# Attention of two decoder layers with its output written already turned, negated logits, four logit buffers and 64-row score tiles

## The chip, the cores and the metric

The kernel runs on one core of a Trainium2 chip. The metric is the device time of one execution in microseconds (us), lower is better. The kernel before takes 1696.79 us, the median of 3 runs (1696.77 to 1696.97). All data are 32-bit floats.

## The reference

One program computes two models one after the other on a sequence of 256 positions of 1024 columns, here worked in two tiles of 128 positions: a first block (feed-forward, three kinds of attention, feed-forward), and then two layers, each with a mixed attention, a cross attention to a memory, and a convolved feed-forward. Only the mixed attention of these two layers and the cross attention behind it are touched. Per layer, from a projection `h` of the input:

```
# latent attention (unit kind M below): 8 heads, causal, values of 64 columns
s = (q_nope . k_nope + q_rope . k_rope) * 96 ** -0.5
o_a = softmax(s where key <= query) @ v
# sparse attention: 8 heads of 64 columns in 2 key groups, three branches
s_c = q . k_compressed * 64 ** -0.5 - slope * distance     # K: 15 compressed keys
s_s = q . k_slc * 64 ** -0.5 - slope * distance            # S: selected keys (all blocks, at 256 positions)
s_w = q . k_win * 64 ** -0.5 - slope * distance            # W: window keys (all, at 256 positions)
o_b = g0 * softmax(s_c) @ v_c + g1 * softmax(s_s) @ v_s + g2 * softmax(s_w) @ v_w
x = layer_norm(ALPHA * x + concat(o_a, o_b) @ w_out)       # 1024 columns
# cross attention (X): 4 heads of 256 columns, 256 memory keys
x = layer_norm(ALPHA * x + softmax(q . k_mem / 16) @ v_mem @ wo)
```

## The kernel before

The kernel names engines directly: each engine has a program of its own, written out in order, and semaphores between them. TensorE (PE) multiplies and transposes, VectorE (DVE) adds biases, takes maxima and divides, ScalarE (ACT) takes exponentials and copies out of PSUM. Large products are worked in a 2 x 2 block scheme of seven products (numbered 1 to 7), whose sums of weights DVE makes.

The mixed attention of a layer is a list of 26 units, UNITS_2: K of tile 0, K of tile 1, then for each tile S0 W0 S1 W1 S2 W2 S3 W3 M0 M1 M2 M3. A unit is one kind, two heads (K: eight) and one tile of 128 queries; in tile 0 it has 128 keys, in tile 1 it has 256. The function `attend` stands three times, once in the program of each engine, and runs over steps j:

- PE (L1180): scores of unit j (L1190), the transposition of the probabilities of unit j-2 (L1206), the product with the values of unit j-3 (L1232). The result is 128 queries x 64 columns for each head, in PSUM.
- DVE (L2322): `logits(j)` adds the bias and takes the row maximum in one instruction for each head (L2357, a custom instruction, with a short one that reads the maximum), then negates the maxima (L2360); `mid` works only for K, B and X units (for X, reciprocal L2378 and two scalings of the probabilities L2382); `output(j-3)` takes the reciprocal of the row sum (L2403), multiplies it with the gate for S and W (L2413), and scales the result out of PSUM into the rows O1 (L2421), for S and W adding to what stands there (L2419).
- ACT (L1678): copies the transposed probabilities of unit j-2 out of PSUM (L1702), then the exponentials of unit j (L1692), each with a short instruction that reads the row sum.

Scores have two buffers in PSUM, logits three in SBUF (`lbuf`), transposed probabilities two in PSUM and two in SBUF (PTS). In the first steps PE also computes quarters of the memory values (L1538), eight passes of 512 columns each. In the trace each product of 32-bit floats shows as two records, a transposition as one.

When the units are done, PE transposes the rows O1 to columns x_t (batches E_O, L1116), ACT copies them out (L1603, L1609), and `shared_product` (L831) multiplies them with w_out: products 1 and 2 need only tile 0, the others need also sums that DVE makes of both tiles (`act_sums_of`). Cross attention runs four units X through the same `attend`.

## Time and profile before

| | |
|---|---|
| median of 3 runs | 1696.79 us |
| the profiled execution | 1696.81 us |
| its span | 1694.9 us |
| TensorE clock granted, of full | 0.998 |
| PE busy | 1665.5 us (98%) |
| PE weight loads busy (beside PE) | 1281.4 us (76%) |
| DVE busy | 1223.2 us (72%) |
| ACT busy | 352.5 us (21%) |
| POOL busy | 212.7 us (13%) |

The profile is one execution. The span goes from the first to the last instruction, and some 1.9 us of the execution's time lie around it. Busy time of PE counts each matmul from its start to a modelled end, so that short waits of PE between two matmuls do not show as idle; the distance between starts shows them. The mixed attention of layer 0 runs from 831.11 to 891.98 us, that of layer 1 from 1312.19 to 1373.05 us.

### The profile page before, as it was taken

The numbers are of one execution on the slowest core, as the hardware profiler recorded it, in microseconds if no ns is written. First come the engines' busy times: TensorE is split into PE (matmuls) and PEld (weight loads), VectorE is DVE, ScalarE is ACT, GpSimd is POOL, SyncE is SP. The second block draws the span as 40 slices with busy tenths as digits, with TensorE's granted clock in tenths as the row PEclk, the third lists the DMA queues.
The fourth block names the chain that finished last, engine by engine and source line by source line (L and its number), as shares of the span: only waits on it lengthen the run. The fifth ranks groups of instructions, "written<-read, shape, count | busy, mean of one in ns | idle before, by whom it ended". The sixth has DMA issues, their size and how long they took to land.

```text
span 1694.9 us, 22817 instructions
## 1 busy us (share of the span) xinstructions
PE 1665.5 (98%) x8726; PEld 1281.4 (76%) x8726; DVE 1223.2 (72%) x2230; ACT 352.5 (21%) x893; POOL 212.7 (13%) x139
## 2 busy tenths in 40 slices
PE   7999999999999999999999999999999999999998
PEld 6887488877847886477784969994687767699953
DVE  6777467976787777573376778996844685789995
ACT  2111000034511111112270212220012531222210
POOL 1222211121021212211001000002120000000021
PEclk9999999999999999999999999999999999999999
DMA  9685454524176555346513536444447206265440
GB/s 320 194 230 177 146 199 162 175 80 149 51 232 213 160 164 184 124 145 178 207 51 131 155 125 194 156 170 153 158 121 252 100 1 224 71 226 177 150 173 25
DMA packets 163755, 267.07 MB, mean 158 GB/s; under 512 B 4279, under 2 KB 106477, under 8 KB 163519
## 3 DMA queue, kind: packets, MB, share of 16 engines
q1 hardware_dynamic: 157902, 248.66, 43.8%
q0 software_dynamic: 5008, 15.91, 3.3%
q8 instruction: 70, 1.15, 0.3%
q10 hardware_dynamic: 736, 1.05, 0.3%
q14 instruction: 39, 0.31, 0.1%
HBM read 262.52 MB, written 2.03 MB: 156 GB/s over the span
## 4 chain that ended last, share of the span: by engine, by line
PE 90%; DVE 5%; DVEq 2%; issue 1%; ACT 1%; DMA 1%; SPq 0%; ACTq 0%
PE psum L1017 19%; PE psum L886 16%; PE psum L1065 13%; PE psum L952 12%; PE psum L844 7%; PE psum L1275 4%; PE psum L1481 3%; PE psum L1538 3%; PE psum L1190 3%; PE psum L1116 3%; PE psum L1232 2%; PE psum L825 2%; PE psum L1104 2%; PE psum L1206 1%; PE psum L1221 1%
## 5 line engine op out<-in xcount | busy, mean ns | idle before, releaser
L695 POOL TENSOR_TENSOR work<-ring,work 128x1024 f32<-128x1024 f32 (+2 forms) x59 | 147.4, 2499 | 791.5 <-DVE work L2199 791.5
L2191 DVE TENSOR_TENSOR work<-ring 128x1024 f32<-128x1024 f32 (+2 forms) x102 | 122.0, 1196 | 83.3 <-PE psum L1065 74.3
L1065 PE MATMUL psum<-ring,work 128*128 128x512 f32 x352 | 160.8, 592 | 0.0
L2195 DVE TENSOR_TENSOR ring<-ring 128x1024 f32<-128x1024 f32 (+2 forms) x104 | 131.7, 1267 | 7.7
L2199 DVE TENSOR_TENSOR work<-ring 128x1024 f32<-128x1024 f32 (+2 forms) x102 | 122.6, 1202 | 7.6
L1065 PEld LDWEIGHTS psum<-ring,work 128*128 128x128 f32 x352 | 66.4, 190 | 81.1 <-issue 79.9
L1065 PE MATMUL psum<-work 128*128 128x512 f32 x264 | 122.5, 592 | 0.0
L1017 PE MATMUL psum<-x_t,work 128*128 128x128 f32 x832 | 101.4, 275 | 0.0
L1017 PE MATMUL psum<-work,ring 128*128 128x128 f32 x832 | 101.4, 275 | 0.0
L1017 PE MATMUL psum<-x_t,ring 128*128 128x128 f32 x832 | 97.4, 275 | 1.6 <-ACT x_t L1610 1.6
L1017 PEld LDWEIGHTS psum<-x_t,work 128*128 128x128 f32 x832 | 97.1, 192 | 0.0
L1017 PEld LDWEIGHTS psum<-work,ring 128*128 128x128 f32 x832 | 97.1, 192 | 0.0
L1017 PEld LDWEIGHTS psum<-x_t,ring 128*128 128x128 f32 x832 | 95.0, 192 | 2.4 <-issue 2.4
L1065 PEld LDWEIGHTS psum<-work 128*128 128x128 f32 x264 | 49.7, 190 | 62.0 <-issue 60.3
L2823 DVE SCALAR_TENSOR_TENSOR work<-work 128x254 f32<-128x254 f32 (+1 forms) x176 | 83.5, 526 | 3.3
L886 PE MATMUL psum<-ring,work 128*128 128x256 f32 x352 | 83.2, 379 | 0.0
L886 PE MATMUL psum<-ring,x_t 128*128 128x256 f32 x352 | 81.7, 386 | 1.5 <-DMA ring<-in_ffn_w_gate_dram 1.3
L886 PE MATMUL psum<-work,x_t 128*128 128x256 f32 x352 | 82.9, 379 | 0.0
L1190 PE MATMUL psum<-work 128*128 128x256 f32 (+2 forms) x384 | 79.5, 338 | 0.3 <-DVE stat L2360 0.3
L886 PEld LDWEIGHTS psum<-ring,x_t 128*128 128x128 f32 x352 | 67.9, 194 | 12.2 <-DMA ring<-in_ffn_w_gate_dram 2.4
L1692 ACT ACTIVATE work<-work,stat 128x256 f32<-128x256 f32 (+1 forms) x136 | 61.6, 453 | 66.5 <-DVE stat L2360 65.6
L886 PEld LDWEIGHTS psum<-ring,work 128*128 128x128 f32 x352 | 66.9, 190 | 9.1
(304 smaller groups left out, 2865.6 us busy)
## 6 DMA issues: line engine op xcount, KB each, us to landing
ring<-in_ffn_w_up_dram SPq DMA_DIRECT2D x66, 1024.0 KB, 7.9
ring<-in_w_in_dram SPq DMA_DIRECT2D x21, 2048.0 KB, 7.9
ring<-in_ffn_w_down_dram SPq DMA_DIRECT2D x20, 2048.0 KB, 7.8
ring<-in_ffn_w_gate_dram SPq DMA_DIRECT2D x22, 1024.0 KB, 5.7
ring<-in_xa_wkv_dram SPq DMA_DIRECT2D x8, 2048.0 KB, 9.5
ring<-in_w_out_dram SPq DMA_DIRECT2D x6, 2048.0 KB, 10.9
ring<-in_xa_wq_dram SPq DMA_DIRECT2D x4, 2048.0 KB, 7.9
ring<-in_xa_wo_dram SPq DMA_DIRECT2D x4, 2048.0 KB, 11.3
```

Source lines behind the costliest of these rows:

```text
L695: nc.gpsimd.tensor_tensor(t4, quarters(n, chunks, pitch)[2], t2, ALU.subtract).then_inc(fourth_ready, 1)
L844: last = mm(share_bank(p), acts[p][:, q, :], rhs[:, i, :], start=(q == 0), stop=(q == KD // 2 - 1))
L886: last = mm(corners(j)[p], acts[p][:, i, :], rhs[:, i, :], start=(i == 0), stop=(i == KD // 2 - 1))
L952: last = mm(row_corners(j)[p][:, 0:pitch // 2], acts[p][:, i, :], rhs[:, i, :], start=(i == 0), stop=(i == KD // 2 - 1))
L1017: last = mm(corners(j)[p][:, c * P:(c + 1) * P], weights[:, i, c * P:(c + 1) * P], acts[p][:, i, :], start=(i == 0), stop=(i == KD // 2 - 1))
L1065: last = mm(sums[p], acts[p][:, q, :], rhs[:, i, :], start=(q == 0), stop=(q == KF // 2 - 1))
L1190: last = mm(PS[:, o:o + x["keys"]], q, k[:, 0:x["keys"]], start=(c == 0), stop=(c == len(pairs) - 1))
L1275: last = mm(row_corners(q + 1)[p], acts_of_gates[p][:, i, :], rhs[:, i, :], start=(i == 0), stop=(i == KD // 2 - 1))
L2191: v.tensor_tensor(t3, b22, b12, ALU.subtract)
L2195: v.tensor_tensor(b12, b12, b11, ALU.subtract)
L2199: v.tensor_tensor(t2, b22, b12, ALU.subtract).then_inc(forms_ready, 1)
L2823: last = v.scalar_tensor_tensor(dst, UP[:, q, 0:T - t], CWT[:, 2 - t, k:k + 1], dst, ALU.mult, ALU.add)
```

## The change

It changes the mixed attention in five ways. (1) The gates and the division by the row sum are put on the probabilities, before they are transposed (`mid`), for all kinds. (2) The product with the values takes the values as the stationary operand and the transposed probabilities as the moving one, for two units at a time: 64 output partitions for each head, so two heads write the halves 0..63 and 64..127 of the partitions. K, S and W of a tile add up in PSUM, and ACT copies the finished 512 columns straight into x_t; the rows O1, their transpositions and `turn_mixed` are gone. (3) The custom instruction gives the negated logits and their minimum, which is the bias of the exponential (scale -1), and L2360 is gone; this holds for X as well. (4) The logits have four buffers, and PE's transposition comes three steps behind the scores instead of two (`ahead=3`), the values four; K of tile 1 stands between the tiles. (5) In tile 1 the scores of S and W of the same heads are issued together, each head with 64 rows instead of 128 (`scores_by_rows`), into four PSUM banks.

On PE in tile 1 of a layer, before, one unit after the other (L1190 scores, L1206 transpositions, L1232 values):

```order
L1190 MATMUL psum<-work 128x256 x2
L1206 MATMUL psum<-ident_fours,work 128x128 x4
L1232 MATMUL psum<-work 128x64 x4
L1190 MATMUL psum<-work 128x256 x2
L1206 MATMUL psum<-ident_fours,work 128x128 x4
L1232 MATMUL psum<-work 128x64 x4
```

and after, S and W (L1196 the scores by rows, L1227 transpositions, L1250 values by halves), first with K of tile 1 (L1238), then the round of S and W as it repeats:

```order
L1227 MATMUL psum<-ident_fours,work 128x128 x4
L1238 MATMUL psum<-work 128x128 x4
L1196 MATMUL psum<-work 128x256 x4
L1227 MATMUL psum<-ident_fours,work 128x128 x8
L1250 MATMUL psum<-work 64x128 x8
L1196 MATMUL psum<-work 128x256 x4
```

Two units now go through PE as one round, and the number of instructions is the same.

At the end of a layer's attention PE has before:

```order
L1206 MATMUL psum<-ident_fours,work 128x128 x4
L1232 MATMUL psum<-work 128x64 x4
L1206 MATMUL psum<-ident_fours,work 128x128 x4
L1232 MATMUL psum<-work 128x64 x8
L1116 MATMUL psum<-ident_fours,work 128x128 x8
L844 MATMUL psum<-ring,x_t 128x512 x4
L1116 MATMUL psum<-ident_fours,work 128x128 x8
```

and after (L848 is the first product of `shared_product`):

```order
L1211 MATMUL psum<-work 128x256 x2
L1227 MATMUL psum<-ident_fours,work 128x128 x4
L1250 MATMUL psum<-work 64x128 x8
L1227 MATMUL psum<-ident_fours,work 128x128 x8
L1250 MATMUL psum<-work 64x128 x8
L1227 MATMUL psum<-ident_fours,work 128x128 x4
L1250 MATMUL psum<-work 64x128 x8
L848 MATMUL psum<-ring,x_t 128x512 x8
```

The sixteen transpositions L1116 are gone, and the values of the last four units come in two lots of eight.

On DVE a unit of tile 1 before (ISA is the custom instruction and its read):

```order
L2357 ISA work,stat<-psum,work 128x256
L2357 ISA stat 128x1
L2357 ISA work,stat<-psum,work 128x256
L2357 ISA stat 128x1
L2360 TENSOR_SCALAR stat<-stat 128x2
L2403 RECIPROCAL stat<-stat 128x2
L2421 TENSOR_SCALAR work<-psum,stat 128x64 x2
```

and after:

```order
L2413 ISA work,stat<-psum,shared 128x256
L2413 ISA stat 128x1
L2413 ISA work,stat<-psum,shared 128x256
L2413 ISA stat 128x1
L2446 RECIPROCAL stat<-stat 128x2
L2457 TENSOR_SCALAR work<-work,stat 128x256 x2
```

The reciprocal now belongs to the unit two steps back, and what follows it scales the probabilities and stands ahead of their transposition.

The core of the diff:

```diff
 def unit(kind, n, tile):
...
+UNITS_2 = [x for i in range(TT) for x in
+           [unit("K", 0, i)] + [unit(k, h, i) for h in range(4) for k in "SW"] + [unit("M", h, i) for h in range(4)]]
+SPARSE_UNITS, TILE_UNITS = 9, 13
...
-            return w(W_L + 512 * (u % 3), 512)
+            return w((W_L, W_L + 512, W_L + 1024, W_O1)[u % 4], 512)
...
 # PE
+                def scores_by_rows(j):
+                    u = u0 + j
+                    pe.wait_ge(group_free, at(H_WV + 2, G_LAYER, l))
+                    pe.wait_ge(logits_ready, at(u, U2, l))
+                    for t in (j, j + 1):
+                        x = units[t]
+                        for s in range(2):
+                            r = slice(HD * s, HD * s + HD)
+                            o = ((u0 + t) % 2) * 1024 + s * x["pitch"]
+                            (q, k), = query(x, s, 1)
+                            last = mm(PS[:, o:o + x["keys"]], q[r], k[r, 0:x["keys"]], start=True, stop=True)
+                        last.then_inc(scores_ready, 1)
...
+                def turned_values(j):
...
+                    if k == "K":
+                        if x["tile"]:
+                            pe.wait_ge(unit_done, at(U1 + SPARSE_UNITS, U2, l))
+                        for c in range(4):
+                            last = mm(PO[:, c * P:(c + 1) * P], VBD[:, c // 2, (c % 2) * P:(c % 2 + 1) * P],
+                                      PTS[:, u % 2, (c // 2) * P:(c // 2 + 1) * P], start=(c == 0), stop=False)
...
+                    for t in (j - 1, j):
+                        y = units[t]
+                        o = (512 if k == "M" else 0) + P * y["n"]
+                        for kb in range(y["nk"]):
+                            for s in range(2):
+                                n = s * y["nk"] + kb
+                                last = mm(PO[HD * s:HD * s + HD, o:o + P], values(y, s, kb), PTS[:, (u0 + t) % 2, n * P:(n + 1) * P], ...
+                    last.then_inc(values_ready, 2)
...
-                for j in range(n + 3):
+                for j in range(n + ahead + 1):
...
                     if j < n:
                         scores(j)
-                    if 0 <= j - 2 < n:
-                        turn(j - 2)
+                    if 0 <= j - ahead < n:
+                        turn(j - ahead)
...
-                        value(j - 3)
+                        value(j - ahead - 1)
...
-                attend(UNITS_2, U1, l, {1 + 2 * i + h: values_between(i, h) ...})
+                attend(UNITS_2, U1, l, {1 + 2 * i + h: values_between(i, h) ...}, ahead=3)
...
-                shared_product(L_OUT, ..., E_O, turn_mixed(E_O, U1 + TT + 12, 19, l), l)
+                shared_product(L_OUT, ..., "O", lambda i: None, l)
 # ACT
-                            last = activation(v, v, ACT.Exp, bias=NM[:, b4, s:s + 1], accum_out=SM[:, b4, s:s + 1])
+                            last = activation(v, v, ACT.Exp, scale=-1.0 if x["kind"] in "SWMX" else 1.0, ...
...
+                def turned_rows_out(j):
+                    act.wait_ge(values_ready, at(u + 1, U2, l))
+                    i, sparse = x["tile"], x["kind"] == "W"
+                    src = PO[:, 0:512] if sparse else PO[:, 512:1024]
+                    dst = XT[:, 4:8, i * P:(i + 1) * P] if sparse else XT[:, 0:4, i * P:(i + 1) * P]
...
-                    if 0 <= j - 2 < n:
-                        out_of_psum(j - 2)
+                    if 0 <= j - ahead < n:
+                        out_of_psum(j - ahead)
...
                         exps(j)
...
+                    if 0 <= j - ahead - 1 < n and units[j - ahead - 1]["kind"] in "WM" and units[j - ahead - 1]["n"] == 3:
+                        turned_rows_out(j - ahead - 1)
...
-                turned_rows(E_O, XT, l)
 # DVE
+                                last = v.tensor_tensor_reduce(out=dst, in0=src, in1=bias_of(x, s), scale=-1.0, scalar=-TAKEN,
+                                                              op0=ALU.add, op1=ALU.min, accum_out=NM[:, b4, s:s + 1])
...
+                    if x["kind"] in "SW":
+                        c = 3 * 2 * x["n"] + (1 if x["kind"] == "S" else 2)
+                        for s in range(2):
+                            last = v.tensor_scalar(L[:, s * n:(s + 1) * n], L[:, s * n:(s + 1) * n], RC[:, b4, s:s + 1],
+                                                   ngate[:, x["tile"], c + 3 * s:c + 3 * s + 1], ALU.mult, ALU.mult)
...
+                    if x["kind"] in "MX":
...
-                    if 0 <= j - 1 < n and j != mid_first:
-                        mid(j - 1)
+                    if 0 <= j - ahead + 1 < n and j != mid_first:
+                        mid(j - ahead + 1)
```

For K, `mid` now also takes the reciprocal, multiplies it with the gate and multiplies the probabilities with it: three more small instructions.

## Rows read from the trace of the kernel before

**Rows 1.** The page's chain that ended last, by engine.

```profile
PE 90%; DVE 5%; DVEq 2%; issue 1%; ACT 1%; DMA 1%; SPq 0%; ACTq 0%
```

**Rows 2.** Windows, layer 0's mixed attention, tile 0 and tile 1: length, busy by engine.

```profile
831.11:863.78 32.67, 31.56 (x165) 21.83 (x164) 17.48 (x105) 14.73 (x57) 0.00 (x0) 1.00 0.36 129
863.78:891.98 28.20, 28.20 (x210) 26.17 (x210) 22.13 (x121) 22.02 (x71) 0.00 (x0) 1.00 0.01 1
```

**Rows 3.** Timeline, tile 0: start us, length us, engine, line, operation, tiles, count.

```profile
850.84 0.61 PE L1190 MATMUL psum<-work 128*128 128x128 f32 x4
...
859.23 0.66 PE L1190 MATMUL psum<-work 128*128 128x128 f32 x4
...
859.80 0.28 DVE L2357 CUSTOM_DVE_ANT_0 work<-psum,shared 128x128 f32<-128x128 f32 x1
...
860.01 0.29 DVE L2357 CUSTOM_DVE_ANT_0 work<-psum,shared 128x128 f32<-128x128 f32 x1
...
860.75 0.66 PE L1190 MATMUL psum<-work 128*128 128x128 f32 x4
```

**Rows 4.** Timeline, tile 1, one step of 256 keys.

```profile
877.50 1.08 PE L1190 MATMUL psum<-work 128*128 128x256 f32 x4
...
878.41 0.60 PE L1206 MATMUL psum<-ident_fours,work 128*128 128x128 f32 x4
...
878.62 0.42 DVE L2357 CUSTOM_DVE_ANT_0 work<-psum,work 128x256 f32<-128x256 f32 x1
...
878.85 1.00 PE L1232 MATMUL psum<-work 128*128 128x64 f32 x8
...
878.96 0.42 DVE L2357 CUSTOM_DVE_ANT_0 work<-psum,work 128x256 f32<-128x256 f32 x1
...
879.69 1.08 PE L1190 MATMUL psum<-work 128*128 128x256 f32 x4
```

**Rows 5.** Timeline, products into 32 output partitions each, and the next full ones.

```profile
801.82 1.95 PE L1493 MATMUL psum<-ring,work 128*32 128x128 f32 x64
803.70 0.70 PE L1481 MATMUL psum<-work,ring 128*128 128x256 f32 x2
```

**Rows 6.** Timeline, the first block: full products, two products of 64 rows, transpositions.

```profile
390.19 0.59 PE L1275 MATMUL psum<-ring,work 128*128 128x256 f32 x2
390.71 0.70 PE L1337 MATMUL psum<-work 64*128 64x256 f32 x4
391.35 0.66 PE L1116 MATMUL psum<-ident_fours,work 128*128 128x128 f32 x4
```

**Rows 7.** Groups by form: count, busy us, mean ns of one, idle us before.

```profile
L2382 DVE TENSOR_SCALAR work<-work,stat 128x256 f32<-128x256 f32 x16 | 4.9, 350 | 0.6
L2387 DVE TENSOR_SCALAR work<-work,stat 128x128 f32<-128x128 f32 x4 | 1.1, 286 | 0.3
L1692 ACT ACTIVATE work<-work,stat 128x256 f32<-128x256 f32 x76 | 38.0, 500 | 51.3 <-DVE stat L2360 50.8
L1702 ACT COPY work<-psum 128x512 f32<-128x512 f32 x34 | 19.8, 582 | 11.6 <-PE psum L1206 11.4
```

**Rows 8.** Timeline, cross attention: reciprocal, scalings and the transposition behind them.

```profile
963.85 0.16 DVE L2378 RECIPROCAL stat<-stat 128x2 f32<-128x2 f32 x1
...
964.09 0.62 DVE L2382 TENSOR_SCALAR work<-work,stat 128x256 f32<-128x256 f32 x2
...
964.76 0.66 PE L1206 MATMUL psum<-ident_fours,work 128*128 128x128 f32 x4 [0.15 <-DVE work L2382]
```

**Rows 9.** Timeline, K of tile 0: first step of its logits, and its exponential.

```profile
832.20 0.27 DVE L2338 MEMSET work<- 128x256 f32 x1 [3.12 <-PE psum L1190]
...
833.58 0.30 ACT L1688 ACTIVATE work<-work 128x120 f32<-128x120 f32 x1 [1.25 <-DVE work L2346]
```

**Rows 10.** Timeline, the first eight of the turned outputs and the product behind them.

```profile
891.98 1.04 PE L1116 MATMUL psum<-ident_fours,work 128*128 128x128 f32 x8
893.15 3.67 PE L844 MATMUL psum<-ring,x_t 128*128 128x512 f32 x8
```

More of the change, by code:

```diff
@@ L228, in unit @@
     subs = 3 if kind == "A" else 4 if kind == "K" else 2
-    return dict(kind=kind, n=n, tile=tile, keys=keys, subs=subs, pitch=512 if kind == "C" else keys, nk=1 if kind == "K" else keys // P,
-                wide=kind == "A", mid=kind in "BKX")
+    return dict(kind=kind, n=n, tile=tile, keys=keys, subs=subs, pitch=512 if kind == "C" or kind in "SW" and tile else keys, nk=1 if kind == "K" else keys // P,
+                wide=kind == "A", mid=kind in "BKSWMX")
 UNITS_1 = [unit("B", h, i) for i in range(TT) for h in range(4)] + \
@@ L1178, in values, with attend @@
                 return KV[:, kb, c:c + HD]
-            def attend(units, u0, l=None, between={}, behind_turn={}):
+            def attend(units, u0, l=None, between={}, behind_turn={}, ahead=2):
+                def scores_by_rows(j):
[10 more added lines that the diff above has]
+                        last.then_inc(scores_ready, 1)
                 def scores(j):
                     x, u = units[j], u0 + j
+                    if x["kind"] in "SW" and x["tile"]:
+                        if x["kind"] == "S":
+                            scores_by_rows(j)
+                        return
                     if j >= 2:
@@ L1224, in value @@
                         return
-                    dv = P if k == "B" else T if k == "K" else HD
-                    blocks = [(s, kb) for s in range({"B": 1, "K": 2}.get(k, x["subs"])) for kb in range(x["nk"])]
+                    dv = P if k == "B" else HD
+                    blocks = [(s, kb) for s in range({"B": 1}.get(k, x["subs"])) for kb in range(x["nk"])]
                     for n, (s, kb) in enumerate(blocks):
@@ L1676, in first_copies, with attend @@
                 hidden(UPS - 1)
-            def attend(units, u0, l=None, between={}, behind_copy={}):
+            def attend(units, u0, l=None, between={}, behind_copy={}, ahead=2):
                 def exps(j):
@@ L1691, in exps @@
                             v = L[:, s * n:(s + 1) * n]
-                            last = activation(v, v, ACT.Exp, bias=NM[:, b4, s:s + 1], accum_out=SM[:, b4, s:s + 1])
+                            last = activation(v, v, ACT.Exp, scale=-1.0 if x["kind"] in "SWMX" else 1.0, bias=NM[:, b4, s:s + 1],
+                                              accum_out=SM[:, b4, s:s + 1])
                         last.then_inc(probs_ready, 1)
@@ L1714, in mixed_rows @@
                         copy(dst, src).then_inc(unit_done, 1)
+                def turned_rows_out(j):
+                    x, u = units[j], u0 + j
+                    act.wait_ge(values_ready, at(u + 1, U2, l))
+                    i, sparse = x["tile"], x["kind"] == "W"
+                    src = PO[:, 0:512] if sparse else PO[:, 512:1024]
+                    src = src.rearrange("p (k t) -> p k t", k=4)
+                    dst = XT[:, 4:8, i * P:(i + 1) * P] if sparse else XT[:, 0:4, i * P:(i + 1) * P]
+                    if not sparse and i == 0:
+                        copy(dst[:, 0:2, :], src[:, 0:2, :]).then_inc(quarter_out, 1)
+                        copy(dst[:, 2:4, :], src[:, 2:4, :]).then_inc(unit_done, TILE_UNITS - SPARSE_UNITS)
+                    else:
+                        copy(dst, src).then_inc(unit_done, SPARSE_UNITS if sparse else TILE_UNITS - SPARSE_UNITS)
                 n = len(units)
-                for j in range(n + 4):
+                for j in range(n + ahead + 2):
                     if j in between:
                         between[j]()
-                    if 0 <= j - 2 < n:
-                        out_of_psum(j - 2)
+                    if 0 <= j - ahead < n:
+                        out_of_psum(j - ahead)
                     if j in behind_copy:
@@ L2320, in bias_of, with attend @@
                 return zero_bias[:, 0:x["keys"]]
-            def attend(units, u0, l=None, between={}, mid_first=None):
+            def attend(units, u0, l=None, between={}, mid_first=None, ahead=2):
                 def logits(j):
@@ L2356, in logits @@
                                 src = dst
[L2357 to L2358 removed]
+                            if x["kind"] in "SWMX":
+                                last = v.tensor_tensor_reduce(out=dst, in0=src, in1=bias_of(x, s), scale=-1.0, scalar=-TAKEN,
+                                                              op0=ALU.add, op1=ALU.min, accum_out=NM[:, b4, s:s + 1])
+                            else:
+                                v.tensor_tensor_reduce(out=dst, in0=src, in1=bias_of(x, s), scale=1.0, scalar=TAKEN,
+                                                       op0=ALU.add, op1=ALU.max, accum_out=MX[:, b4, s:s + 1])
+                        if x["kind"] in "SWMX":
+                            last.then_inc(logits_ready, 1)
+                            return
                     dr()
```

89 lines of the change are left out of this document (43 added, 46 removed).

## The prediction

> **What bounds the kernel now.** I read the page's chain first: nine tenths of it are PE [rows 1], so an edit is worth what it takes from the distance between PE's starts. The change touches PE only in the mixed attention of the two layers and behind it, so I read that stretch of layer 0 by windows and then by timeline. It lasts 32.67 + 28.20 = 60.87 us [rows 2], and layer 1's the same. The reader is to see two regimes. With tile 0's 128 keys, a step takes 860.75 - 859.23 = 1.52 us [rows 3]; the scores, transpositions and values in it are some 1.1 us of PE's work, and DVE works without a gap: DVE sets the step. With 256 keys (tile 1), PE starts one group as the other ends: 877.50 to 879.69, 2.19 us, of which scores .91, transpositions .44, values .84 [rows 4]. There PE sets it.
>
> **Cost of the new pieces.** All in us.
>
> *Values into half the output partitions.* The nearest rows are 64 records with a quarter of the partitions each: 803.70 - 801.82 = 1.88 for 64, .029 each [rows 5], where one transposition of the same 128 columns takes .11 (.44 for four, rows 4). So four such tiles run beside each other, and I take two to do so: sixteen records (two units of tile 1) cost 8 x .109 = .87, and with going into and out of that mode 1.09. The mode costs .09 each way: in rows 6 a full product of 256 columns takes .216, two end at 390.62, and the 64-row ones start at 390.71. For tile 0's eight records, .44 + .21 = .65. Before, two units took 1.68 and some .95. Bounds: nothing for the modes (.87), or no overlap at all (16 x .109 + .21 = 1.95). I take 1.09, by the row nearest in kind.
>
> The Trainium skill (TensorE: Matmul & The Clock Gate, Part 3, The mechanism) says that weight loads overlap with running products only when they go to another group of rows. Both halves of a head pair use all rows, so by that rule they would not overlap, and the stage would come out as in the third rival. The trace disagrees with it as far as it goes: the products of rows 5 share all 128 rows too, and take .029 each.
>
> *Scores by rows.* Two products of 64 rows and 256 columns (four records) take 391.35 - 390.71 = .64 [rows 6], against .86 for four full records. A round of S and W has eight: I take two more steps of .216, so 1.06, against 1.84 before. The first unit's scores reach DVE .75 after the start (.33 to its last record, and .42 behind that one, as a full unit's last record, some .70 after 877.50, stands .42 ahead of DVE in rows 4); a full unit's reach it after 1.12 [rows 4].
>
> *DVE.* A logits pair takes .35 + .34 = .69 with 256 keys [rows 4] and .42 with 128 [rows 3]. The negation behind it goes. The new `mid` with 256 keys is what X has: reciprocal at 963.85, transposition freed at 964.76, .91 [rows 8]. With 128 keys it is .77, since a scaling then takes 286 instead of 350 ns [rows 7]. The scalings of S and W have two per-partition scalars instead of one; no row shows that. From 128 to 256 columns the one-scalar form grows by .064, the custom instruction by .14 (.28 to .42). Bounds: no dearer, or dearer by that difference. I take no dearer. Whether the reciprocal starts right behind the custom instruction's read or .07 later is open too.
>
> **The sum for one layer.** The question is what waits on what. PE transposes S of the last pair only when DVE has scaled it, and DVE does this behind the logits of the new S, which wait for its scores. So a round is a chain that crosses from PE to DVE and back, and the values stand behind it:
>
> 1. First five steps: K of tile 1 leaves them (scores .81, transposition .22, values .87) and one unit's scores come (.44): -1.46. The first five end at 850.84 [rows 3], so 850.84 - 831.11 = 19.73 becomes 18.27.
> 2. Tile 0, the other eight units, four rounds: scores to DVE .57 [rows 3], logits .42, scaling .77, transposition .27 (.22 and .05 of start behind a wait), values .65: 2.68 a round, 10.72. Before, nine units took 863.78 - 850.84 = 12.94.
> 3. K of tile 1, no longer under the memory values: its scores reach DVE after 1.10 and its logits take 833.58 - 832.20 = 1.38 [rows 9] before PE may overwrite PSUM with the next burst: 2.48. Then two bursts to the first regular round: .75 + logits .69, scaling of a 128-key M .66, logits .69, K's six small operations 1.77 (of rows 9's kind, .23 to .37 each), logits .69, scaling .91, transposition .49, K's values .87: 7.5.
> 4. Two rounds of S and W: .75 + .69 + .91 + .49 + 1.09 = 3.93, twice 7.86. PE's own work in it would be 1.06 + .87 + 1.09 = 3.0: PE waits some .8 of each. Before, 4.38.
> 5. Two rounds in which M's full scores start the chain: 1.12 + .69 + .91 + .49 + 1.09 = 4.30, twice 8.60.
> 6. The tail. The SBUF buffers of transposed probabilities are two, and a unit is copied into one only when the pair before has been multiplied; ACT works in order. From the end of one pair's values: .13, copy .50, exponentials of the last unit 1.01 (two of 500 ns), the sparse half of x_t .50, copy .66, values 1.09; then .13, copy .50, copy .66, values 1.09 [rows 7]: 6.27.
>
> Sum 18.27 + 10.72 + 2.48 + 7.5 + 7.86 + 8.60 + 6.27 = 61.7, against 60.87: +.8. PE works some 10 us less a layer, and waits it all away again: the round trip through DVE, K without its cover, and ACT's copies at the end.
>
> What is saved outside. The sixteen transpositions of the rows: 893.15 - 891.98 = 1.17 for the first eight with a wait, .87 for the others: -2.04 [rows 10]. Nothing takes their place: product 1 and 2 of tile 0 (sixteen records of .43, 6.9 us) cover ACT's copy of tile 1's columns, and DVE, done with the units some 3 us earlier than PE, makes its sums of tile 1 in that time. Cross attention loses the negation ahead of its first transposition, where PE waits .3: -.24 (bounds 0 and -.3). The four buffers cost nothing themselves; ACT's work stays.
>
> One layer: +.8 - 2.04 - .24 = -1.4. Two: -2.8. Against the profiled execution's 1696.81 (span 1694.9 and what lies around it; the median of the runs is 1696.79, the same within .02) this gives **1694.0 us**.
>
> **Rivals.**
>
> *The dearer scalings.* If two scalars cost DVE the custom instruction's rate (+.07 and +.14 an instruction), each S and W round grows by .13 or .28, and so do the rounds beside them: +1.5 a layer, 1697.0. With the reciprocal .07 later everywhere (+.75 a layer), 1698.5. For it: no row has the form. Against: the one-scalar form with 256 columns takes 350 ns, less than anything that reads two tensors.
>
> *PE stays the bound.* If DVE came back early enough (for instance because the first half of a burst is ready sooner than by rows 6), PE's waits would shrink. With no wait at all, ten us a layer and the 2.3 outside, 1672; with half of them gone, 1682. For it: PE is what the page shows as the bound, and its work falls by a fifth. Against: the chain of point 4 is made of rows, and its order is fixed in the programs.
>
> *The halves don't run beside each other*, the slower side. Then values cost 1.95 a round of tile 1 instead of 1.09, and 1.09 instead of .65 in tile 0, with all of this in the chain: +7 a layer, 1708. It decides from .066 us a record instead of .055, where the gain is gone. For it: no row shows two tiles of 64. Against: rows 5.
>
> *The row bursts do nothing* (a burst as long as before): only S's readiness counts, .75 becomes 1.12; +.4 to +.7 a layer, 1695.
>
> **How the numbers follow.** Within .2%, 3.4 us, is what a measurement of this kernel can tell from no change: 1693.4 to 1700.2. The chain as summed (with the row bursts either way) .66, by itself 1690.5 to 1697: its modes may cost nothing (-1.9 a layer), its starts behind a wait more. It lies across the bound, .32 faster, .32 the same, .02 slower. The dearer scalings .14 (.11 the same, .03 slower). PE as the bound, wholly or in part, .13, faster. The halves one after the other .07, slower. Together faster .45, same .43, slower .12. The range leaves out the third rival and most of the second: 1689 to 1698.6.
>
> **What would show it.** In the trace after: values of two tile 1 units in about 1.1 us (1.95 would be the third rival); the burst's second transposition lot freed by DVE's scaling, with a wait of some .8 on PE; rounds of 3.9 and 4.3 us; a gap of two to three us of PE behind K of tile 1; and two waits of PE for ACT's copy, 1.5 and .9, ahead of the last two lots of values. The stretch from K's scores to the first product should be 61 to 62 us, against 60.87 + 2.04. Scalings of S and W of more than 400 ns would be the first rival. I am wrong in kind, and not only in size, if the rounds of tile 1 are near PE's own 3.0 us, or if PE waits for something else than DVE there.

## The result, and the profile after

The changed kernel takes 1699.84 us in the median of 22 runs (1698.01 to 1701.10), the kernel before 1696.96 us in the median of 22 runs beside it (1696.48 to 1698.17): ratio 1.0016, 95% interval 1.0009 to 1.0022. It is slower by 2.9 us, where 1694.0 had been forecast; the range ended at 1698.6. The profiled execution took 1699.37 us (span 1697.6).

The windows of the mixed attention, tile 0 and tile 1 of layer 0 and then of layer 1, to be read against [rows 2] (length, busy by engine, then the granted clock, which is the third number from the right):

```profile
830.93:861.18 30.25, 27.17 (x149) 17.30 (x147) 14.77 (x88) 14.05 (x57) 0.00 (x0) 1.00 0.39 140
861.18:894.78 33.60, 27.56 (x234) 20.15 (x232) 24.96 (x106) 22.62 (x74) 0.00 (x0) 0.95 0.00 1
1312.73:1342.85 30.12, 27.18 (x149) 17.30 (x147) 14.68 (x88) 14.05 (x57) 0.00 (x0) 1.00 0.40 140
1342.85:1377.62 34.77, 28.96 (x234) 20.84 (x232) 24.98 (x106) 22.53 (x74) 0.00 (x0) 0.90 0.00 1
```

The reader is to see three things. The stage takes 63.9 us in layer 0 and 64.9 in layer 1, not 61.7. The layers differ by 1 us, though they run the same program. And the granted clock is below 1.00 in tile 1, as it was nowhere in [rows 2]. Finer windows of the same kernel find the place:

```profile
862.20:863.80 1.60, 0.31 (x3) 0.07 (x2) 1.19 (x5) 1.09 (x5) 0.00 (x0) 1.00 0.00 0
...
865.20:868.50 3.30, 3.30 (x18) 2.20 (x18) 2.84 (x16) 1.83 (x7) 0.00 (x0) 0.50 0.00 0
...
1343.90:1345.50 1.60, 0.28 (x3) 0.04 (x1) 1.19 (x5) 1.09 (x5) 0.00 (x0) 1.00 0.00 0
...
1346.40:1353.20 6.80, 6.80 (x36) 3.95 (x33) 5.92 (x31) 2.89 (x12) 0.00 (x0) 0.50 0.01 2
```

PE does nearly nothing for 1.6 us behind K of tile 1, and 1 to 1.5 us later it is granted half its clock (the lower of its two levels, 1.2 GHz), for 3.3 us in layer 0 and for 6.8 us in layer 1.

A round of tile 0 in the timeline of PE, and DVE's part of it (start, length, engine, line, operation, tiles, count; in brackets the idle time before and who ended it):

```profile
855.24 0.71 PE L1211 MATMUL psum<-work 128*128 128x128 f32 x4
855.79 0.38 PE L1227 MATMUL psum<-ident_fours,work 128*128 128x128 f32 x2
856.01 0.61 PE L1211 MATMUL psum<-work 128*128 128x128 f32 x4
857.32 0.44 PE L1227 MATMUL psum<-ident_fours,work 128*128 128x128 f32 x2 [0.70 <-DVE work L2451]
857.68 0.66 PE L1250 MATMUL psum<-work 128*64 128x128 f32 x8
858.27 0.71 PE L1211 MATMUL psum<-work 128*128 128x128 f32 x4
```
```profile
855.99 0.29 DVE L2413 CUSTOM_DVE_ANT_0 work<-psum,shared 128x128 f32<-128x128 f32 x1 [0.59 <-PE psum L1211]
...
856.42 0.16 DVE L2446 RECIPROCAL stat<-stat 128x2 f32<-128x2 f32 x1
856.66 0.60 DVE L2451 TENSOR_SCALAR work<-work,stat 128x128 f32<-128x128 f32 x2
```

Where DVE never waited in [rows 3], it now waits .59 us for scores, and PE .70 for DVE: a loop of both, 858.27 - 855.24 = 3.03 us for two units, no shorter than two steps of 1.52 before. Tile 1, one round of S and W, one of M, and the tail:

```profile
871.60 1.13 PE L1196 MATMUL psum<-work 64*128 64x256 f32 x8
872.66 0.66 PE L1227 MATMUL psum<-ident_fours,work 128*128 128x128 f32 x4
874.07 0.66 PE L1227 MATMUL psum<-ident_fours,work 128*128 128x128 f32 x4 [0.75 <-DVE work L2451]
874.65 1.09 PE L1250 MATMUL psum<-work 128*64 128x128 f32 x16
875.68 1.13 PE L1196 MATMUL psum<-work 64*128 64x256 f32 x8
...
884.27 1.13 PE L1211 MATMUL psum<-work 128*128 128x256 f32 x4
...
887.62 1.09 PE L1250 MATMUL psum<-work 128*64 128x128 f32 x16
888.65 0.66 PE L1227 MATMUL psum<-ident_fours,work 128*128 128x128 f32 x4
...
891.40 1.09 PE L1250 MATMUL psum<-work 128*64 128x128 f32 x16 [1.23 <-ACT work L1743]
...
893.76 1.09 PE L1250 MATMUL psum<-work 128*64 128x128 f32 x16 [0.68 <-ACT work L1743]
894.78 1.55 PE L848 MATMUL psum<-ring,x_t 128*128 128x512 f32 x3
```

Where [rows 4] have no idle time of PE at all, every round has some now. The scalings by form answer to [rows 7] (count, busy us, mean ns of one, idle before); the first two have two per-partition scalars, the last two have one:

```profile
L2451 DVE TENSOR_SCALAR work<-work,stat 128x256 f32<-128x256 f32 x16 | 5.9, 410 | 0.6
L2451 DVE TENSOR_SCALAR work<-work,stat 128x128 f32<-128x128 f32 x14 | 4.3, 345 | 0.6
...
L2457 DVE TENSOR_SCALAR work<-work,stat 128x256 f32<-128x256 f32 x8 | 2.5, 350 | 0.3
...
L2457 DVE TENSOR_SCALAR work<-work,stat 128x128 f32<-128x128 f32 x8 | 1.9, 284 | 0.3
```

### The profile page after: what moved, and what is told of

Same layout as the page of the kernel before. It is cut to its first block, busy times and chain, and to the rows that moved or that the text cites. A ratio compares the mean times of both kernels' runs of the same rounds, so it can differ in the third digit from the quotient of the medians.

```text
span 1697.6 us, 22577 instructions
## 1 busy us (share of the span) xinstructions
PE 1653.5 (97%) x8710; PEld 1258.3 (74%) x8710; DVE 1214.2 (72%) x2142; ACT 348.7 (21%) x893; POOL 212.7 (13%) x139
## 4 chain that ended last, share of the span: by engine, by line
PE 90%; DVE 6%; DVEq 1%; issue 1%; ACT 1%; DMA 0%; SPq 0%; ACTq 0%
PE psum L1021 19%; PE psum L890 16%; PE psum L1069 13%; PE psum L956 12%; PE psum L848 7%; PE psum L1324 3%; PE psum L1521 3%; PE psum L1578 3%; PE psum L1120 3%; PE psum L1211 2%; PE psum L829 2%; PE psum L1108 2%; PE psum L1227 1%; PE psum L1250 1%; PE psum L1270 1%
## 5 line engine op out<-in xcount | busy, mean ns | idle before, releaser
L1643 ACT ACTIVATE work<-psum 128x512 f32<-128x512 f32 (+4 forms) x66 | 34.7, 550 | 180.5 <-PE psum L1120 180.3
```

## Experiments

Each run has its median and the span of its runs; "stage" is the length in layer 0 and in layer 1 of the profiled execution, from the small products that stand 7.91 us ahead of K's scores to the start of the last record of the output product (before 94.51 and 94.50, changed kernel 95.48 and 96.51). The changed kernel has 22 runs, e3 ten, e11 to e14 five each, the others eleven. Unless said otherwise an edit is made in the changed kernel.

| run | median us (runs) | ratio to before, 95% | stage |
|---|---|---|---|
| changed kernel | 1699.84 (1698.01 to 1701.10) | 1.0016 (1.0009 to 1.0022) | 95.48, 96.51 |
| e1 values first | 1698.67 (1696.26 to 1700.41) | 1.0008 (1.0000 to 1.0017) | 96.70, 92.94 |
| e2 K between | 1699.86 (1698.50 to 1703.26) | 1.0016 (1.0007 to 1.0025) | 96.86, 95.49 |
| e3 full scores | 1701.29 (1701.09 to 1701.69) | 1.0025 (1.0016 to 1.0034) | 96.92, 96.78 |
| e4 fill gap | 1700.57 (1700.30 to 1701.93) | 1.0021 (1.0012 to 1.0030) | 96.55, 96.43 |
| e5 fill short | 1698.45 (1698.09 to 1699.19) | 1.0008 (1.0000 to 1.0017) | 95.38, 95.25 |
| e6 and one scalar | 1696.77 | 0.9999 (0.9990 to 1.0008) | 94.60, 94.40 |
| e7 values first, full | 1695.05 (1691.82 to 1698.08) | 0.9986 (0.9977 to 0.9995) | 92.28, 92.28 |
| e8 rows by unit | 1696.73 (1691.75 to 1697.57) | 0.9991 (0.9982 to 1.0000) | 94.86, 94.85 |
| e9 before, negated | 1693.24 (1693.11 to 1694.03) | 0.9978 (0.9969 to 0.9987) | 92.87, 92.68 |
| e10 memory late | 1697.56 (1696.93 to 1702.80) | 1.0009 (1.0000 to 1.0018) | 94.17, 95.16 |
| e11 short tail | 1691.35 (1689.91 to 1692.79) | 0.9968 (0.9955 to 0.9980) | 91.77, 92.84 |
| e12 its rows | 1690.00 (1688.14 to 1692.46) | 0.9960 (0.9947 to 0.9972) | 92.87, 91.63 |
| e13 copy first | 1686.80 (1686.27 to 1687.05) | 0.9940 (0.9926 to 0.9953) | 89.50, 89.50 |
| e14 its rows | 1686.44 (1686.24 to 1687.74) | 0.9939 (0.9926 to 0.9951) | 89.29, 89.30 |

### e1: PE's values ahead of the waited transposition

```
-    if 0 <= j - ahead < n: turn(j - ahead)
-    if 0 <= j - ahead - 1: value(j - ahead - 1)
+    if ahead == 3 and 0 <= j - ahead - 1: value(j - ahead - 1)
+    if 0 <= j - ahead < n: turn(j - ahead)
```

> PE's program alone is changed: in each step of the mixed attention the values of the pair before go ahead of the waited transposition instead of behind it. Theory A (the loop scores, logits, scaling, transposition, values, scores sets the rounds, and the values are in it for nothing): a tile 0 round falls from 3.0 us to DVE's own 2.4, a tile 1 round of S and W from 4.09 to about 3.2 (DVE), one of M from 4.44 to PE's own 3.8; some 5 to 6.5 us a layer, 1687 to 1690 against 1699.8. Theory B (the other two engines are as full as PE: ACT's copy of W, 1.5 us of ACT a unit, comes too late and the values now wait for it): under 1 us a layer, 1698 to 1700. The clock should not fall, or fall for a shorter time, if A holds, since PE's waits get shorter.

The profiled execution holds the answer twice. In layer 1 a tile 0 round is 1338.31 - 1335.79 = 2.52 us, a round of S and W 1357.46 - 1353.45 = 4.01, one of M 3.82. That is theory A for tile 0 and M. For S and W it is theory B, since the values now wait for ACT:

```profile
1353.45 1.13 PE L1196 MATMUL psum<-work 64*128 64x256 f32 x8
...
1355.85 1.09 PE L1250 MATMUL psum<-work 128*64 128x128 f32 x16 [0.68 <-ACT work L1745]
...
1357.46 1.14 PE L1196 MATMUL psum<-work 64*128 64x256 f32 x8
```

Layer 0, the same program, takes 3.76 us more. K's region and the tail in layer 0, then in layer 1:

```profile
863.10:871.30 8.20, 7.02 (x39) 4.53 (x39) 5.75 (x29) 3.34 (x13) 0.00 (x0) 0.58 0.00 0
887.90:896.00 8.10, 5.46 (x46) 4.25 (x46) 6.75 (x14) 3.71 (x9) 0.00 (x0) 0.79 0.01 2
...
1346.20:1352.00 5.80, 4.69 (x39) 3.02 (x39) 4.92 (x25) 3.31 (x13) 0.00 (x0) 1.00 0.01 3
1368.50:1375.70 7.20, 4.51 (x51) 3.44 (x49) 5.95 (x14) 3.61 (x9) 0.00 (x0) 1.00 0.00 0
```

At 1.00 the first takes 5.8 us instead of 8.2. So with the clock held the order of the waits is worth 2.3 us in a layer (92.94 against e5's 95.25 below; the 3.6 from layer 1's own 96.51 hold the clock's cost too), and the low clock takes that back in the other. The last sentence of the expectation, that the clock should not fall, was wrong: the rounds' waits got shorter, but K's stayed (1.36 us idle in the timeline's brackets; the expectations count from start to start, 1.63), and the tail's grew from 1.23 to 1.82.

### e2: K of tile 1 between the second and third M of tile 0

```
-    [unit("K", 0, i)] + [S and W of tile i] + [unit("M", h, i) for h in range(4)]
+    tile 0: ... M0, M1, unit("K", 0, 1), M2, M3;  tile 1: without its K
```

> The unit K of tile 1 goes between the second and the third M of tile 0 instead of behind the fourth. Theory A (K without cover costs PE its 1.63 us wait, and that wait brings the lower clock of the next 3 to 7 us): the wait behind K shrinks to under 1 us and PE stays at the full clock; -1.5 to -3 us a layer, 1694 to 1697. Theory B (K's logits and six small operations, 3.2 us of DVE, are work that DVE has to do in any place, and DVE and the chain through it are the bound there too): the wait only moves; 1699 to 1700.

Theory B: the wait only moved. Layer 0 of this run:

```profile
859.64 0.61 PE L1212 MATMUL psum<-work 128*128 128x128 f32 x4
861.70 0.69 PE L1228 MATMUL psum<-ident_fours,work 128*128 128x128 f32 x2 [1.45 <-DVE work L2458]
```

Behind it the clock is .53 from 861.70 to 865.20; in layer 1, with the same wait, it stays at 1.00.

### e3: full-row scores in tile 1

```
-    if x["kind"] in "SW" and x["tile"]: (one burst of both units, 64 rows)
+    (each unit in its own step, like M)
```

> Tile 1's S and W are scored unit by unit in full-row products, as M is, instead of in one burst of 64-row products a pair. Theory A (a round is a loop through DVE, and PE's work in it that isn't on the loop is free): the loop's first link is then .37 us longer (scores reach DVE 1.12 instead of .75 after the start), as M's rounds show, 4.44 against 4.09: four S and W pairs, +1.2 to +1.6 us a layer, 1702 to 1703. Theory B (the burst does nothing, since it makes the second unit's scores wait with the first's): within 0.3 us a layer, 1699.3 to 1700.4. Theory C (the burst harms: it ties two units together): faster than 1699.

Theory A in the stage: a round of S and W is 881.45 - 876.95 = 4.50 us instead of 4.09, and the stage 1.5 us longer than with the clock held (e5). The burst was worth what the forecast gave it. The clock held here (1.00 in both layers, all runs within .6 us), so that the total rose by 1.45 only and not to the 1702 of theory A; I had not expected that, since PE waits 1.46 us for DVE's work on K here too.

### e4 and e5: work in the gap behind K

```
     if j == TILE_UNITS + 1:
         pe.wait_ge(logits_ready, at(u - 1, U2, l))
+        for _ in range(6):      # e5: range(3)
+            mm(PS[:, (u % 2) * 1024:(u % 2) * 1024 + T], KTM[:, 0, 0:P], KTM[:, 0, :], start=True, stop=True)
```

> Six products of 256 columns (1.3 us of PE work, results unused and overwritten) are put into PE's 1.63 us wait behind K of tile 1, nothing else is changed. Theory A (that wait is what brings the granted clock of 0.50 in the 3.3 us from 865.2 in layer 0 and the 6.8 us from 1346.4 in layer 1, and the low clock costs the steps there): granted clock 1.00 through both layers, 10.4 and 11.6 us from K to the first regular round become 10.0 both: 0.4 + 1.6, 1697.5 to 1698.5. Theory B (tile 0's waits of .85 to 1.1 us in each round of 3 us bring the low clock as well, or instead): the dip stays or moves, 1699 to 1700.5. Theory C (the dip costs nothing because PE waits for DVE anyway): clock 1.00 and 1699.5 or more.

I had counted one record a product; the six were twelve records and 2.69 us, 1.1 us too long: the burst began at 864.97 instead of 863.87. The clock was 1.00 in both layers, and layer 1 no longer lost to layer 0. The size needed the shorter fill:

> As the run with filled gap, with three products in place of six. There each turned out to be two records, so that the six took 2.69 us where 1.5 had been free, and the burst behind started 1.16 us later; the clock stayed at 1.00 in both layers and the runs lay within 1.6 us. Theory A (the waits around K bring the low clock, and the low clock costs what layer 1 lost on layer 0, plus a little in both): clock 1.00, stage to the product's end 95.3 us in both layers (95.48 and 96.51 in the changed kernel), 1698.2 to 1698.6. Theory B (the low clock costs nothing, since PE waits there anyway): 1699.5 or more. Theory C (1.3 us of work are too little to hold the clock): dips in the trace, and a spread of the runs like the changed kernel's.

Theory A: 1698.45 us, both windows around K at 1.00, and the runs within 1.1 us where the changed kernel's lie within 3.1.

```profile
860.00:875.00 15.00, 12.24 (x95) 8.75 (x93) 11.60 (x60) 10.56 (x41) 0.00 (x0) 1.00 0.01 2
1342.00:1357.00 15.00, 12.15 (x95) 8.65 (x94) 11.74 (x62) 10.55 (x41) 0.00 (x0) 1.00 0.01 2
```

The low clock costs 1699.84 - 1698.45 = 1.4 us in the median, and work without use in an idle gap gives it back. The changed kernel's own runs say the same without any edit: of the five with a mean granted clock of .998 or .999 four took 1698.01 to 1698.66 us (one 1699.73), and the twelve with .995 or .996 took 1699.37 to 1701.10.

### e6: one scalar instead of two

e6 is e5, and leaves the gate out of S and W.

```
-    ..., RC[:, b4, s:s + 1], ngate[...], ALU.mult, ALU.mult)
+    ..., RC[:, b4, s:s + 1], None, ALU.mult)
```

> The short fill, and the scalings of S and W without their second per-partition scalar (the gate isn't applied to these branches). To be compared with the short fill alone. Theory A (the second scalar costs .06 us an instruction, and one unit's pair of scalings in each round is on the loop): a round of S and W falls by .12, eight rounds a layer, M's rounds stay: -0.9 us a layer, -1.8. Theory B (both units' scalings count, because DVE has no slack): -1.9 a layer, -3.8. Theory C (the loop doesn't run through the scalings): no change.

Theory A, nearly to the digit: 1698.45 - 1696.77 = 1.7 us. (Ten runs lie between 1696.43 and 1697.18; one took 4453.78.) The scalings of S and W take 352 and 284 ns here, 410 and 345 with two scalars.

### e7 and e8: values first, with full scores, and with 64 rows unit by unit

e7 is e1 and e3 together. e8 is e1 and, in the scores of tile 1:

```
-    pe.wait_ge(logits_ready, at(u, U2, l))
-    for t in (j, j + 1):
+    pe.wait_ge(logits_ready, at(u - 1, U2, l))
+    for t in (j,):
...
-    if x["kind"] == "S": scores_by_rows(j)
+    scores_by_rows(j)
```

> The values ahead of the waited transposition, and tile 1's S and W in full-row products unit by unit. With values first alone a tile 1 round of S and W was 4.01 us (PE waits .83 for ACT's copy of W's transposed probabilities, which it has only just turned) and one of M 3.81. Theory A (PE's own work is then the round, for S and W as for M): 3.8 each, no wait of PE over .4 us in tile 1, and so no low clock in tile 1's rounds: stage 92.5 us in both layers, 1692.5 to 1695. Theory B (as in the run with full scores alone, the longer scores are on the loop): +.4 a round, 94 to 95 us, 1696 to 1698.

> The values first, and tile 1's S and W in 64-row products, but each unit's own two products in its own step, not two units in one burst. Theory A (a unit's two 64-row products take .64 us as two products did in rows 6, .87 or more in full rows; PE's round is then 2 x .64 + .88 + 1.02 = 3.2, which is also DVE's 3.16): rounds of 3.3 us, stage 91 us, 1690 to 1693. K's wait shrinks by .7 us, since S's scores no longer wait for K's logits. Theory B (DVE's two-scalar scalings and ACT's 1.5 us a unit keep the round near 3.8, whatever PE does): 92.5 us, 1693 to 1695. In both, more waiting of PE than with full scores: low clock stretches could cost either 1 to 3 us a layer, and would show in the spread of the runs.

e7 is theory A in the profile (all rounds of tile 1 3.82 us, 92.28 us in both layers), and only in part in the median. Its runs lie 6.3 us apart and follow the clock: the four with a mean granted clock of .999 took 1691.82 to 1692.56 us, the two with .994 and .995 took 1697.98 and 1698.08. Long waits were left in it, 1.34 us at the first W and 1.82 in the tail:

```profile
888.29 1.09 PE L1248 MATMUL psum<-work 128*64 128x128 f32 x16 [1.82 <-ACT work L1743]
```

e8 is theory B in its rounds, which are 3.82 us too, but took longer than either theory said. What PE saves in scores it waits for ACT's copy of W, and behind the tail's wait the clock was .50 for 6.8 us in both layers (888.6 to 895.4 and 1369.8 to 1376.6), which is the 94.9 against 92.3: up to the tail the two run alike.

### e9: the kernel before, with the negated logits alone

This holds for S, W, M and X; the exponential takes the scale -1, and the negation L2360 is gone for them.

```
-    v.tensor_tensor_reduce(..., scale=1.0, scalar=TAKEN, op1=ALU.max, accum_out=MX[...])   then NM = -MX
+    v.tensor_tensor_reduce(..., scale=-1.0, scalar=-TAKEN, op1=ALU.min, accum_out=NM[...])
```

> The kernel before with one part of the change alone: S, W, M and X write negated logits and take the minimum, so that the small negation behind them goes. Theory A (tile 0's step of 1.52 us is DVE's, rows 3, and the negation is .24 us of it; tile 1 is PE's own and gains nothing): 1.28 to 1.35 a step, nine steps, -1.5 to -2.1 us a layer, and -.24 in the cross attention: 1692.3 to 1693.6. Theory B (with DVE's share gone the step is soon held by another engine, or by the loop through it): -.5 a layer, 1696.

Theory A: a step of tile 0 is mostly 1.28 us instead of the 1.52 of [rows 3], PE has no wait over .3 us, and the kernel takes 1693.24 us, 3.9 less than the kernel before beside it (1697.10):

```profile
858.61 0.66 PE L1190 MATMUL psum<-work 128*128 128x128 f32 x4
...
859.88 0.66 PE L1190 MATMUL psum<-work 128*128 128x128 f32 x4
```

This one part does more than the whole change was forecast to do. The other parts, as they were put together, cost 1699.84 - 1693.24 = 6.6 us.

### e10 to e12: ACT's copies

e10 is e7, with the copies of the memory values moved from unit 5 to unit 13. e11 adds the short tail; e12 is e11 with e8's scores:

```
-    attend(UNITS_2, U1, l, {5: lambda: memory_values(0, (1, 3), 2)}, ahead=3)
+    attend(UNITS_2, U1, l, {TILE_UNITS: lambda: memory_values(0, (1, 3), 2)}, ahead=3)
     e11:
+    return w((W_PTS, W_PTS + 512, W_PTS + 1024, W_O1 + 512)[u % 4], 512)    # four PTS buffers
+    (ACT) if ahead == 3 and j == n - 1: exps(j)      ahead of out_of_psum
+    (ACT) turned_rows_out of tile 1's last W at step n + ahead - 1
+    (PE)  value(n - 3) at step n + 2, behind turn(n - 1)
```

> The run with values first and full scores (1695.05, profiled run 1690.8 in span), and in it ACT's two copies of the memory values out of PSUM moved from unit 5 to unit 13 (K of tile 1). There PE waited 1.39 us (850.75 to 852.36, less the usual .22) for ACT's copy of the first W, behind these two copies of 1.05 us. Theory A: PE's wait falls to .4, -1.0 us a layer; S of tile 1 waits for the moved copies by .3, hidden in K's wait. 1693. Theory B (DVE is late there by as much, so that the wait stays): 1695. Either way the tail's waits (2.1 and 1.0 us) keep bringing the low clock in part of the runs, and the spread stays near 6 us.

> As the run with late memory copies, and at the end of the attention: four SBUF buffers for the transposed probabilities instead of two, ACT does the last unit's exponentials before a copy, and the sparse half of x_t behind the last copy; PE transposes the third and fourth M of tile 1 before it multiplies the first two. Theory A (the tail is ACT's chain of copies): the waits of 2.1 and 1.0 us become 1.2 and under .5, -2.0 to -2.5 us a layer, and without them the clock holds in nearly all runs: 1686 to 1689, spread under 3 us. Theory B (the clock is lost elsewhere): -2 a layer in the profile, but a median over 1690 and a spread of 5 us.

> As the run before it, with tile 1's S and W in 64-row products, each unit in its own step, instead of full rows. In the pair of runs without the other edits both had rounds of 3.82 us: with 64 rows PE does .5 us less work in a round and waits it for ACT's copy of W. Theory A (only waits are added): the stage takes the same time, but PE idles more, so the clock falls in more of the runs: 1687 to 1691, above its neighbour. Theory B (with four buffers the copy comes earlier, and the rounds fall to 3.4): 1684 to 1687, below its neighbour.

e10 missed: the wait at the first W did fall to .4 us, but the copies now held up the PSUM that tile 1's first scores need, and the clock fell behind that in layer 1 (in layer 0 behind the tail's wait). e11 has the same wait, and took 1691.35 us where theory A said 1686 to 1689:

```profile
862.65 1.65 PE L1212 MATMUL psum<-work 128*128 128x256 f32 x3 [1.62 <-ACT work L2004]
```
```profile
860.70:862.60 1.90, 0.33 (x3) 0.09 (x2) 1.40 (x7) 1.90 (x7) 0.00 (x0) 0.94 0.00 0
862.60:864.60 2.00, 1.95 (x4) 1.17 (x4) 0.28 (x2) 0.47 (x2) 0.00 (x0) 0.50 0.00 0
```

The tail itself shrank as expected, from 892.16 - 885.01 = 7.15 us in e7 to 4.82 in e11. e12 against e11 decides nothing: their runs overlap.

### e13 and e14: the copies in unit 5, behind the copy of the first W

e13 is e11, and e14 is e12, with:

```
-    attend(UNITS_2, U1, l, {TILE_UNITS: lambda: memory_values(0, (1, 3), 2)}, ahead=3)
+    attend(UNITS_2, U1, l, {}, {5: lambda: memory_values(0, (1, 3), 2)}, ahead=3)
```

> As the run with full scores and the short tail, but ACT copies the memory values behind its copy of the first W, in unit 5, and not in unit 13. In unit 13 the copies (1.08 us, begun at 861.50) freed PSUM for S of tile 1 only at 862.6, PE waited 1.9 us there and the clock fell. Theory A (the low clock comes where PE waits over 1.5 us, and each of the two layers now has no such wait): PE's wait at the first W is .4 as with the late copies, K's wait is spread over four of under .9 us; stage 89 us in both layers, clock 1.00, runs 1685 to 1687.5 with a spread under 3 us. Theory B (waits of .3 to .9 us in every round are enough for the low clock): the profiled stage as in A where the clock holds, but a median above 1688 and a spread of 5 us.

> The same with tile 1's S and W in 64-row products, each unit in its own step. Theory A (PE then waits .4 us more in each round for ACT's copy of W, and nothing is gained in time): stage as its neighbour's within .5 us, more low clock, a median 1 to 3 us above its neighbour's. Theory B (K's region, where DVE sets the pace, gains by earlier scores): up to .7 us a layer better than its neighbour.

Theory A of e13: from the first W to the product PE has no wait over .7 us (line waited for: us in total, times, longest), 1.00 in both layers, five runs within .8 us, 1686.80. The tail of e13 begins at 883.89, and the product starts at 888.70:

```profile
PE psum L1251 <- ACT work L1751: 1.6, 4, 0.7
PE psum L1228 <- DVE work L2456: 0.6, 1, 0.6
```
```profile
830.82:859.67 28.85, 26.94 (x150) 17.34 (x149) 14.50 (x87) 13.89 (x57) 0.00 (x0) 1.00 0.42 147
859.67:888.70 29.03, 27.60 (x234) 21.73 (x232) 24.17 (x106) 22.75 (x74) 0.00 (x0) 1.00 0.01 1
```
```profile
883.89 1.45 PE L1228 MATMUL psum<-ident_fours,work 128*128 128x128 f32 x8
...
888.70 0.70 PE L851 MATMUL psum<-ring,x_t 128*128 128x512 f32 x1
```

e14 is .2 us a layer better in the stage (theory B's direction, a third of its size), and within the runs' span of e13. Both beat the kernel before by 10 us, ratio .994. e14 holds all five parts of the change, its 64-row scores unit by unit and not in one burst; e13 does without the 64-row scores. Against the changed kernel's 63.9 us from K's scores to the product, e13 takes 57.9 us.

## Why the prediction was wrong

What was right. Outside the stage all held: the product follows without the sixteen transpositions (56 records in one piece, -2.0 us), and the stretch from it to the cross attention's product went from 57.74 to 57.50 us, -.24. The halves run beside each other: sixteen records in 1.03 us against 1.09, so the third rival is out. By the rule of the Trainium skill (TensorE: Matmul & The Clock Gate, Part 3, The mechanism), that weight loads overlap with running products only on another group of rows, the halves would have gone one after the other. The trace disagrees: two halves of the output partitions that share all rows take .055 us a record, half of .11. The burst's worth was right (e3). PE waits .75 in S and W rounds where .8 stood, 1.23 and .68 in the tail where 1.5 and .9 stood, but only 1.36 behind K where two to three had been said.

The steps, forecast against layer 0 and layer 1:

| step | forecast | measured |
|---|---|---|
| 1. first five steps | 18.27 | 18.23, 18.23 |
| 2. tile 0's four rounds | 10.72 | 12.03, 11.89 |
| 3. K to the first regular round | 9.98 | 10.41, 11.58 |
| 4. two rounds of S and W | 7.86 | 8.17, 8.17 |
| 5. two rounds of M | 8.60 | 8.88, 8.89 |
| 6. tail | 6.27 | 6.14, 6.14 |

Sum 63.86 and 64.90 against 61.7. The mechanism was right, the chain from PE through DVE and back. Three of its terms were mis-sized, and one thing was not seen.

- Step 2 failed most, 1.2 to 1.3 us a layer. In the round shown above the chain's links are .75 + .43 + .90 + .37 + .59, where .57 + .42 + .77 + .27 + .65 was forecast.
- "Scores to DVE .57 [rows 3]" is a misread row. DVE set the step there, and its logits at 859.80 belong to the unit before. The kernel before shows it where tile 1 begins: the scores with 256 keys start at 863.78, but the next logits still have 128 keys, and those with 256 come only at 865.63. Where DVE stood idle and waited for scores, the link is .64:

```profile
844.35 0.61 PE L1190 MATMUL psum<-work 128*128 128x128 f32 x4
844.99 0.29 DVE L2357 CUSTOM_DVE_ANT_0 work<-psum,work 128x128 f32<-128x128 f32 x1 [2.54 <-PE psum L1190]
...
863.78 1.08 PE L1190 MATMUL psum<-work 128*128 128x256 f32 x4
...
864.35 0.28 DVE L2357 CUSTOM_DVE_ANT_0 work<-psum,shared 128x128 f32<-128x128 f32 x1
...
865.63 0.41 DVE L2357 CUSTOM_DVE_ANT_0 work<-psum,work 128x256 f32<-128x256 f32 x1
```

- The passages. The other .1 of the scores' link and the .1 by which the values start later both lie where PE passes between half-column products and full ones. I had .21 for both passages together, from the 64-row products of [rows 6], and put it into the values. In tile 0 the two transpositions, the eight records of values and the four of scores behind them (the next transposition starts at 858.82) take 858.82 - 857.32 = 1.50 us; by .11, .055 and .11 a record they would be 1.10. Of the .4 some .05 is the start behind a wait, which the old program has too, and .35 goes into the two passages. That this is the price of the passage is read from the traces alone; no run took it away.
- "I take no dearer", for the scalings with two scalars. They cost .06 us each in both widths, 345 to 284 and 410 to 350 ns, below the bounds' upper end in tile 1 and near it in tile 0. e6 sizes this at 1.7 us for the kernel. It is the first rival with a bit over half its price; I had given it .14.
- The clock. No rival had it, though the forecast itself named a gap of 2 to 3 us behind K. It costs 1.4 us in the median (e5), and explains why layer 1 is 1 us longer than layer 0 and why the runs spread.

Two layers, with what lies outside the stage: +2.5 us in the profiled execution against -2.8, a miss of 5.3. The scalings are 1.7 of it and the clock 1.4; the misread link is .6 (.07 in each of eight rounds of tile 0). The remaining 1.6 is what the passages between the two modes would be (.14 a round in tile 0 above the .21 forecast, less in tile 1), which is argued and not shown.

The larger oversight isn't in the sum. I took the order of PE's program as given, and so had the values in the loop and ACT's copies at its end, and I weighed only "PE waits it all away". e9 shows that the one part that shortens DVE, without any new loop, was worth 3.9 us; e14, that the five parts are worth 10 once the values come first, the tail is reordered with two more buffers, and ACT's copies are moved. Whether all three are needed was not tried apart from each other: the short tail without the moved copies was not run, nor the copies in unit 5 without it. The halves, the four logit buffers and the 64-row scores were not run alone in the kernel before either.

## What to carry to other kernels

When a change takes work from the engine that sets the pace and adds waits to it, sum the waits as a loop through all engines, and ask of each piece in the loop whether it must be there: here the values stood behind a wait that they did not need. Read the length of a link only where the engine at its end was idle and waited; a row in which that engine is late says nothing about it. Price the idle time of TensorE twice, as time and as the clock that may fall behind it; a spread of the runs that grows from 1.7 to 3.1 us is the sign to look for stretches of granted clock .50. And run the parts of a change alone: the negated logits alone were worth more than the whole as first put together.

## What was unexpected of the hardware

- The low clock did not follow a wait for certain. Behind waits of 1.4 to 1.8 us it came in one layer and not in the other of one execution (e1, e2), and in e3 it stayed at 1.00 in both layers through a wait of 1.46 us and one of 1.2. With no wait of PE over .7 us it came in none (e13), and the five runs lay within .8 us. In the changed kernel it lasted 3.3 us in one layer and 6.8 in the other, and in e12 10.2 (862.0 to 872.2).
- The work that pays needn't be the work that waited: in e8 .50 came behind the tail's wait for ACT and lasted into the output product, whose 56 records took 25.1 us instead of 24.1.
- Two per-partition scalars instead of one cost a tensor-scalar instruction of DVE .06 us at 128 columns (284 to 345 ns) as at 256 (350 to 410 ns), so a fixed price and not a rate.
